# Early gate products in the attentions: whole halves in every fifth or sixth step instead of one or two portions in each

## The reference, cut to what matters

```python
def block_sweep_attention(q, k, v, scale, forget_cum):
    for start in range(0, s_len, Q_BLOCK):          # Q_BLOCK = 128
        end = start + Q_BLOCK
        logits = einsum('bqhd,bkhd->bhqk', q[:, start:end], k[:, :end]) * scale
        ...                                         # masked; with forget_cum added in the second
        p = softmax(logits)
        outs.append(einsum('bhqk,bkhd->bqhd', p, v[:, :end]))

for i in range(N_BRANCHES):
    gate = sigmoid(h @ w_gate[i] + b_gate[i])
    merged = merged + gate * (branches[i] @ w_branch_up[i])
```

## Time and profile before

| | |
|---|---|
| median of 3 runs | 3099.35 us (3096.55 to 3099.67) |
| the profiled execution | 3094.74 us |
| its span, first to last instruction | 3093.0 us |
| mean granted TensorE clock | 0.966 of full |
| PE busy | 2818.3 us (91%) |
| DVE busy | 1431.7 us (46%) |
| ACT busy | 952.0 us (31%) |
| POOL busy | 121.2 us (4%) |

### The profile page before, as it was taken

How to read it: one execution, slowest core, us unless ns; L and a number is a source line. 1 busy time by engine, 2 the same in 40 slices (tenths; PEclk the granted TensorE clock), 3 DMA queues, 4 the chain that set the end, 5 groups by cost and what they waited for, 6 DMA issues and landing times. The chain is left out here.

```text
span 3093.0 us, 35149 instructions
## 1 busy us (share of the span) xinstructions
PE 2818.3 (91%) x14648; PEld 2196.2 (71%) x14648; DVE 1431.7 (46%) x1621; ACT 952.0 (31%) x1291; POOL 121.2 (4%) x185
## 2 busy tenths in 40 slices
PE   6999998889978898987999999999389989999988
PEld 5767776567756676775888888888177768877776
DVE  2164442533142234846433434233746779842943
ACT  3141122333122433433323323121236622223122
POOL 0001110000000200100000100000000000000000
PEclk9999999999999999998999999999699999999999
DMA  3120011101112104621333333111320121112331
GB/s 105 43 74 32 29 39 56 55 29 48 52 47 72 49 23 159 212 63 48 109 96 96 102 96 98 53 48 48 122 75 28 48 68 58 52 41 96 106 116 68
DMA packets 66095, 220.81 MB, mean 71 GB/s; under 512 B 7608, under 2 KB 12504, under 8 KB 64288
## 3 DMA queue, kind: packets, MB, share of 16 engines
q1 hardware_dynamic: 51552, 165.01, 16.2%
q0 software_dynamic: 14400, 53.75, 5.1%
HBM read 179.93 MB, written 38.80 MB: 71 GB/s over the span
## 5 line engine op out<-in xcount | busy, mean ns | idle before, releaser
L280 PE MATMUL psum<-mixer_in,weights_parts 128*128 128x512 f32 x2112 | 504.4, 399 | 19.2 <-PEq L184 16.4
L280 PEld LDWEIGHTS psum<-mixer_in,weights_parts 128*128 128x128 f32 x2112 | 398.5, 189 | 118.4 <-issue 17.8
L424 PE MATMUL psum<-hidden,weights_parts 128*128 128x512 f32 x1536 | 433.8, 424 | 41.7 <-ACT early_gate L448 22.1
L247 DVE TENSOR_TENSOR weights_parts<-weights_raw,weights_parts 128x1024 fp32r<-128x1024 f32 (+2 forms) x195 | 211.4, 1084 | 386.7 <-ACT weights_parts L231 386.5
L424 PEld LDWEIGHTS psum<-hidden,weights_parts 128*128 128x128 f32 x1536 | 286.0, 195 | 127.4 <-issue 33.3
L280 PE MATMUL psum<-mlp_in,weights_parts 128*128 128x512 f32 x1536 | 352.3, 391 | 1.5 <-PEq L2418 1.5
L280 PE MATMUL psum<-mlp_hidden,weights_parts 128*128 128x512 f32 x1536 | 352.2, 391 | 0.0
L280 PEld LDWEIGHTS psum<-mlp_in,weights_parts 128*128 128x128 f32 x1536 | 288.4, 188 | 65.3 <-issue 2.3
L280 PEld LDWEIGHTS psum<-mlp_hidden,weights_parts 128*128 128x128 f32 x1536 | 288.5, 188 | 63.1
L280 PE MATMUL psum<-hidden,weights_parts 128*128 128x512 f32 x1200 | 279.2, 395 | 11.4 <-PEq L812 6.6
L231 ACT CAST weights_parts<-weights_raw 128x1024 fp32r<-128x1024 f32 (+2 forms) x195 | 182.2, 935 | 337.9 <-PE psum L280 223.7
(11 more groups left out here) (450 smaller groups left out, 3212.8 us busy)
## 6 DMA issues: line engine op xcount, KB each, us to landing
weights_raw<-in_w_in SPq DMA_DIRECT2D x73, 512.0 KB, 3.6
weights_raw<-in_w_mlp SPq DMA_DIRECT2D x64, 512.0 KB, 3.6
mod_weights<-in_mod_w POOLq DMA_DIRECT2D x80, 256.0 KB, 3.8
weights_raw<-in_w_gate SPq DMA_DIRECT2D x32, 512.0 KB, 3.7
gate_scratch<-early_gate SPq DMA_DIRECT2D x64, 256.0 KB, 2.2
gate<-gate_scratch POOLq DMA_DIRECT2D x32, 512.0 KB, 4.2
weights_raw<-in_w_out SPq DMA_DIRECT2D x24, 512.0 KB, 3.6
x_tokens<-in_x SPq DMA_DIRECT2D x4, 1024.0 KB, 8.1
```

Of the source, the lines that this page charges most:

```text
L247: nc.vector.tensor_tensor(c.parts[:, s, 1, 0:w], c.raw[:, s, 0:w], c.parts[:, s, 0, 0:w].bitcast(F32), ALU.subtract).then_inc(c.low_ready, 1)
L280: mm = nc.tensor.matmul(c.psum[:, bank + h, 0:cols], c.parts[:, s, wp, at], moving(k, xp, h), start=(n < halves), stop=(n >= halves * (3 * ...
L424: mm = nc.tensor.matmul(c.psum[:, bank, :], c.parts[:, s, wp, at], self.hidden[:, k, xp, h * HALF:(h + 1) * HALF], start=(k == 0 and n == ...
```

## The change

The list `ends` says how many of the 48 portions are multiplied by the end of step n. Before, it grows by one or two portions in every step. After, it is rounded down to a whole half (8 portions, 24 matmuls).

```diff
-        ends, at = [], 0
+        ends = []
         for n in range(len(turns) + 1):
-            to = portions * (n + 1) // (len(turns) + 1)
-            at = min(to, (at // KT + 1) * KT)
-            ends.append(at)
+            ends.append(portions * (n + 1) // (len(turns) + 1) // KT * KT)
```

## The result

The changed kernel is slower: 3126.60 us, median of 4 runs (3125.47 to 3127.86), against 3097.97 for the kernel before in the same comparison (3096.55 to 3099.67). The ratio is 1.0092, with a 95% interval of 1.0075 to 1.0110.

A forecast was written before the change was run, and what follows sets the result against it. PE was taken as nearly the bound, with chains between engines ruling many steps. Terms -1.2 + 0.4 + 8.4 + 2.1 + 3.6 + 3.4 = +16.7 us on 3099.35 gave 3116, range 3103 to 3128.

The forecast's parts named there:

- the two prices W and C: Per step: PE's own work without early portions (4.33 us in block 7), and the transposes-to-exponential chain PE cannot shorten (4.52).
- The wait for the copy: PE's idle for ACT's copy of early gates at L424 goes from 3.8 us to 0 in each attention.
- Steps with a half: Steps 10, 16, 21, 27 run at PE's pace: 7.2, 8.0, 8.7, 9.6 us, together 33.5.
- Steps 6 to 31: Sum of 108.2 us per attention: -1.2 us in the first, +0.4 in the second.
- The end: Step 32 has 24 early matmuls instead of 6, all on the path: +4.2 us in each attention.
- The beginning: Steps 1 to 5 take 13.9 and 14.3 us, the half starting at half clock speed: +2.1 and +3.6.
- The clock at step 13: PE idles 2.7 us; a 3.4 us low-clock stretch in steps 14 and 15 costs 1.7 us per attention, +3.4.
- The other idle steps: Steps 9, 17, 24, 25 and 29, idle 1.5 to 1.7 us, were counted as bringing no low clock.
- B: Rival: steps without portions run at PE's own pace, clock stays up at step 13; 3104 us, chance 0.16.
- rival C: Low clock after all five further steps idle over 1.5 us: 3133, chance 0.11; mild form, some of them, 3124 to 3130, 0.08.
- The idle for exponentials: PE's idle at L2190 was to rise from 6.3 to some 20 us an attention.

The follow-up runs named there:

- the filler everywhere: Changed kernel plus matmuls with unused results in steps 9, 13, 17, 24, 25, 29 and 31, where PE idles over 1 us: 3115.40 us.
- the portions by slack: Against the changed kernel, portions given by what each step's chain can hide, last half whole in step 32: 3077.56 us, ratio 0.9944 to the kernel before.
- the undoing: Changed kernel with the first half spread over steps 0 to 5 as before, the other five halves whole: 3122.01 us.
- halves at the ends of blocks: Changed kernel with its whole halves moved to steps 5, 9, 13, 17, 25 and 29, none at the end: 3101.35 us.
- the low part later: Changed kernel with DVE making its early low parts two turns later (turns 14 and 25, not 12 and 23): 3117.13 us.

## Why the prediction was right or wrong, point by point

- **What bounds, and the two prices W and C.** Right, and shown. Every step of after in which the clock is up lies within 0.5 us of the forecast, and most within 0.1; four later kernels were forecast from the same two prices and came out in their medians within 3 us of the times written down. The steps are the better test: steps 6 to 31 took 108.9 us for 108.8 with the filler everywhere, and 95.1 for 95.5 with the portions by slack.
- **The wait for the copy.** Right: it goes (3.8 to 0.0 us), and alone it is worth 8.8 us in the two attentions, where 9 were said, but only if the clock is held up.
- **Steps with a half.** Right: 7.2, 7.9 (with the clock up), 8.6, 9.6, where 7.2, 8.0, 8.7, 9.6 were said.
- **Steps 6 to 31.** 108.2 was said for the chains; 108.9 shown with the filler everywhere. In the change itself it was 113.7, for the clock.
- **The end.** The +4.2 us is right in the second attention (4.11 to 8.24). In the first it is +7.3, since the clock fell after step 31, where no clock was counted.
- **The beginning.** Said +2.1 and +3.6; measured +2.3 and +3.6, and the undoing gave -2.5 and -3.7. The parts as printed add up to 13.75 and 14.15 us, 0.15 less than the 13.9 and 14.3 that went into the sum; measured were 14.15 and 14.3.
- **The clock at step 13: the step that failed.** The mechanism and the place were right, the size was not: 1.7 us was put for each attention, and it was 4.9 in each (17.46 and 17.51 us for 12.57 in steps 14 to 16). I took the length of the low stretch, 3.4 us, from the one row of before, and it was three times as long, 10.2 us. This term was short by 6.4 us. In the row of before six early matmuls followed the idle, here transposes, values and scores alone; but whether that makes the length is not shown. Behind step 21 of the kernel with halves at the ends of blocks such work followed too, and the stretch was 3.4 us; with the beginning spread, one stretch after step 13 lasted 13.7 us, its last 2.9 under the early matmuls of step 16.
- **The other idle steps.** "1.84 us is the smallest idle that I saw" was true and a bad bound, and even that idle brought the low clock in one attention of before and not in the other. In steps 6 to 31 of the ten profiled executions the clock fell, within 2 us of the end of the idle, after none of 14 idle times of 0.99 to 1.18 us, after 6 of 46 of 1.27 to 1.45, after 7 of 10 of 1.75, and after all four of 2.48. The length of the idle is not all: the 1.36 us in step 17 brought it in two of two attentions where portions in ones and twos stood before, and in none of eight where a whole half stood directly before. In the change's profiled execution it fell once at the end, +3.2 us; the prediction left step 31 out of the steps that might, though it has no scores to multiply and its idle is the second longest.
- **The rivals.** B (steps at PE's pace) is refuted: the chains stand. C (low stretches after steps 9, 17, 24, 25 and 29) was not so in the profiled execution, where none of the ten came; the one further fall was after step 31, which I had not listed. But other kernels had it behind steps 9, 17, 21 and 25, so C was a danger, not a certainty.
- **What the profile would show.** The idle for exponentials was to be some 20 us and is 14.5: I added the idle of starts, while the page counts from the modelled end of a matmul (in step 13, 2.7 against 2.48). At a low clock PE also looks busy where it waited.
- **Sum.** Of the 27.4 us in the two attentions 16.7 were forecast, 6.4 are the clock at step 13, 3.2 the clock at the end, and 1.1 the small rest. The medians differ by 28.6, and the 1.2 us more is not resolved: the parts outside the attentions differ by more than that from one execution to the next. That the time still lay in the range is owed to the room that the range had for a mild form of rival C, not to the term of the clock.

## What to carry to other kernels

Filler work in a chain that alternates between engines should be given out by what each step's wait can hide, not evenly and not in lumps: with the same 48 portions the medians were 3126.6, 3095.5 to 3098.0, or 3077.6 us. A wait that a change removes has to be priced together with the idle time that it leaves on PE, since an idle of 1.35 to 2.5 us cost up to five more at the lower clock in some of these attentions, and nothing in others. A low stretch of one trace is one case: look for its twins, with the same idle, before its length or its coming is put into a sum.

## What the runs showed of the hardware that I had not expected

- After the idle of 2.48 us in step 13 the granted clock fell in all four attentions of the two profiled kernels that had it unfilled, at once or within 2 us. It stayed at 0.5 for 10.2 us in the changed kernel, while PE was busy 9.98 of them with transposes, 64-column products and scores. In the kernel before, with early matmuls directly behind, it was 3.4 us, and 3.4 us as well in one place with such thin work alone behind it (PE busy 3.40 of 3.40 us, halves at the ends of blocks).
- The same idle, with the same kinds and numbers of instructions around it, was followed by half clock in one attention and by full clock in the other of the same execution: 1.35 us in step 13 with the low part later, and 1.84 us in step 17 of the kernel before. Why is open; only the profiled executions show it.
- Ten matmuls whose results nobody reads, put in such an idle, shortened the next three steps by 4.9 us and cost the step itself nothing (4.67 us with and without).
